# The low parts of split weights, made by GpSimd in pieces of 512 columns

## Chip, cores and metric

The kernel runs on one core of a Trainium2 chip. The metric is the device time of one execution in microseconds (us). The time before is the median of three runs; the trace is one more execution, taken by the hardware profiler. TensorE is called PE below (PEld is its weight load), VectorE is DVE, ScalarE is ACT, GpSimd is POOL, SyncE is SP.

## What is computed

Two transformer blocks stand behind one another, A and B, of two layers each, on 512 tokens of 1024 features, all in float32. Cut to what matters here:

```python
# block A, one layer
h = modulate(rms_norm(x, g1), sh1, sc1)
proj = h @ w_in                       # 1024 x 5152: queries, keys, values, gates
a = gla_chunked(...)                  # gated linear attention, two directions
b = diff_attention(...)               # softmax(p0) - lam * softmax(p1), 4 heads
x = x + g1 * ((sigmoid(ga) * (a @ w_a) + sigmoid(gb) * (b @ w_b)) @ w_o)
x = x + g2 * hier_moe(modulate(rms_norm(x, g2n), sh2, sc2))   # 32 experts, top 2
# block B, one layer
p = rmsnorm(x, n1) @ w_in             # 1024 x 2048
x = x + concat(attention, spatial_gating, conv) @ w_out
up = dwconv3(rmsnorm(x, n2) @ ffn_w_up)               # 1024 x 5632
x = x + (silu(gate) * val) @ ffn_w_down               # 2816 x 1024
```

## The kernel before

Activations lie with features on the 128 partitions and the 512 tokens along a row. The weights of a product come from HBM in **blocks** of 2 MB (128 partitions x 4096 columns of float32; the blocks of the down projection have 2816 columns, two of the up projection 2048, the first block of A 256). SP loads them into `ring`, a buffer of slots.

The large products are made in split form. A float32 matrix is written as a high part (rounded to float32r, the format that PE multiplies in one pass) and a low part, which is what the rounding dropped. PE then sums three products: high by high, low by high, high by low. For a block of weights n of these lists (`SPLIT_A` with 11 blocks for each layer of A, `SPLIT_B` with 26 for each layer of B):

- ACT makes the high part by a copy from `ring` into `parts`, slot 4 or 5 by turns (`high_part`, a copy of 3.6 us for 4096 columns), and raises `weights_high_a` or `weights_high`.
- POOL waits for that, and makes the low part: `ring` minus the high part, written over the block in its ring slot, whose name in float32r is also `parts` (`low_part`, lines 757 and 847). It raises `weights_low_a` or `weights_low`.
- PE waits for both before the first product with that block (`block_parts`).

The high part of block n waits until PE has finished block n-2, so ACT and POOL work about one block ahead of PE. Low parts of activations are made by DVE in the same way, 512 columns at a time (lines 1568, 1937, 2032, 2039).

Every engine runs a list of instructions in program order, and the order is written by hand. What stands around the low parts:

- In A, the differential attention takes 16 steps (4 heads x 4 row tiles). In step i DVE adds the bias and takes the maxima (L1685), negates them (L1688: 2 columns), and then scales step i-1 by its sums (L1693 to L1696); ACT takes the exponentials (L2208) between; PE turns the result (L1114). The products with blocks `ga` and `gb` stand between the steps. POOL also issues the DMAs of the bias tables.
- In B, the attention takes 16 steps j: PE makes the scores, DVE takes the maxima (L1975) and scales and negates them (L1977: 2 columns, two operands in SBUF), ACT takes the exponentials (L2372), PE turns them (L1409). Products with blocks `("in", 3)` and `("in", 2)` are spread over the steps; their results leave PSUM by a copy on ACT that stands behind the exponentials in ACT's list. POOL issues the DMAs of tables behind the low parts of its first two blocks (lines 852 and below), and PE waits for all of them before its first `rope_swap`.
- In the feed-forward part of B, DVE makes the hidden rows (L2048, L2049 and L2052) and their low parts (L2039), of which PE takes one after another in the first product of the down projection.

Two of the lines that the change touches, from A and from B:

```python
pool.wait_ge(weights_high_a.sem, weights_high_a.at(l, n + 1))
pool.tensor_tensor(parts[:, s, 0:size], ring[:, s, 0:size], parts[:, 4 + n % 2, 0:size].bitcast(F32),
                   ALU.subtract).then_inc(weights_low_a.sem, weights_low_a.more())
```

Of the kernel before, what the change touches and what calls it, by code (L numbers as in the profile page):

```python
# [27 lines left out]
ALU = mybir.AluOpType  # L28
ACT = mybir.ActivationFunctionType
F32R = mybir.dt.float32r  # L30
F32 = mybir.dt.float32
# [252 lines left out]
def size_b(name):  # L284

    return {"up": lambda j: 2 * P * UPS[j][1] * KD, "dn": lambda j: KF * P}.get(name[0], lambda j: SLOT)(name[1])
# [36 lines left out]
def program(nc, ctx, inp, out):  # L323
    def sb(name, shape, dt=F32):
        return ctx.enter_context(nc.sbuf_tensor("s_" + name, shape, dt))
# [12 lines left out]
    ring = sb("ring", [P, RING, SLOT])  # L338
    parts = nc.alloc_sbuf_tensor_at("s_parts", [P, RING, SLOT], F32R, offset=at)
# [119 lines left out]
    def sig(name, per, credit=0):  # L459
        return Signal(sem(name), per, credit)  # L460
# [25 lines left out]
    weights_high_a, weights_low_a = sig("a_weights_high", len(SPLIT_A)), sig("a_weights_low", len(SPLIT_A))  # L486
# [35 lines left out]
    weights_high, weights_low = sig("b_weights_high", len(SPLIT_B)), sig("b_weights_low", len(SPLIT_B))  # L522
# [21 lines left out]
    def settle(eng):  # L544

        eng.sem_inc(settled, 1)
# [123 lines left out]
    def _(pool):  # L670
        n = [0]
# [59 lines left out]
        def rows(src):  # L731
            return src.rearrange("(k p) -> k p", p=P)

        def small(signal, dst, src):
            pool.dma_start(dst, src).then_inc(signal.sem, signal.more(16))

        with pool.Fori(0, DEPTH) as l:
# [13 lines left out]
            def low_part(n):  # L751

                size = KD * 2 * RANK if n == 0 else SLOT
                s = RA.slot(SPLIT_A[n])
                pool.wait_ge(weights_high_a.sem, weights_high_a.at(l, n + 1))
                settle(pool)
                pool.tensor_tensor(parts[:, s, 0:size], ring[:, s, 0:size], parts[:, 4 + n % 2, 0:size].bitcast(F32),  # L757
                                   ALU.subtract).then_inc(weights_low_a.sem, weights_low_a.more())


            for n in range(7):
                low_part(n)

            for h in range(HEADS):
                if h >= 2:
                    low_part(5 + h)
                if h < 2:

                    pool.wait_ge(TA.done.sem, TA.done_at(l, ("o", 1, 1)))
                else:  # L770
                    pool.wait_ge(TA.by(("L", NT * (h - 1) - 1, 1)).sem, TA.freed_at(l, ("L", NT * (h - 1) - 1, 1)))
                settle(pool)
                row = rel_dram[h, 0:1, P - 1:P - 1 + REL_W]
                small(relm_in[h], relm[h % 2], bass.AP(tensor=row.tensor, offset=row.offset, ap=[[REL_N - 1, P], [1, REL_W]]))

            low_part(9)
            pool.wait_ge(TA.done.sem, TA.done_at(l, ("L", HEADS * NT - 1, 1)))
            settle(pool)
# [49 lines left out]
        with pool.Fori(0, DEPTH) as l:  # L828

            pool.wait_ge(TB.done.sem, l * TB.done.per + (TB.index[("par", 1)] + 1))  # L830
            settle(pool)
            for c in range(2):
                small(params_in_b, prow[44 * c:44 * c + 44, 0, :], rows(inp["ffn_conv_w_2"][l, c]))
            small(params_in_b, prow[0:44, 1, :], rows(inp["ffn_conv_w_2"][l, 2]))
            small(params_in_b, prow[44:52, 1, :], rows(inp["norm1_g_2"][l]))
            small(params_in_b, prow[52:60, 1, :], rows(inp["norm2_g_2"][l]))
            for r, name in ((60, "q_norm_g_2"), (61, "k_norm_g_2")):
                for c in range(2):
                    small(params_in_b, prow[r:r + 1, 1, 64 * c:64 * c + 64], inp[name][l].rearrange("(k p) -> k p", k=1))
            small(params_in_b, prow[62:68, 1, :], inp["conv_w_2"][l].rearrange("t (k p) -> (t k) p", p=P))  # L840

            def low_part(n):

                s, size = RB.slot(SPLIT_B[n]), size_b(SPLIT_B[n])
                pool.wait_ge(weights_high.sem, weights_high.at(l, n + 1))
                settle(pool)
                pool.tensor_tensor(parts[:, s, 0:size], ring[:, s, 0:size], parts[:, 4 + n % 2, 0:size].bitcast(F32),  # L847
                                   ALU.subtract).then_inc(weights_low.sem, weights_low.more())

            low_part(0)  # L850

            pool.wait_ge(TB.freed["V"].sem, TB.freed["V"].at(l, 0))
            settle(pool)
            small(tables_in, swap, inp["swap"])
            small(tables_in, sin_t, inp["rope"][1])
            small(tables_in, cos_t, inp["rope"][0])
            low_part(1)
            small(tables_in, wsr, inp["sg_w_2"][l].rearrange("h p q -> p h q"))
            for h in range(4):
                small(tables_in, bsb[64 * (h % 2):64 * (h % 2) + 64, h // 2, :], inp["sg_b_2"][l, h].partition_broadcast(64))  # L860
            small(tables_in, gvb, inp["sg_norm_g_2"][l].partition_broadcast(P))
            for n in range(2, len(SPLIT_B)):
                low_part(n)
# [1618 lines left out]
```

## Time and profile before

| | |
|---|---|
| median of three runs | 3723.69 us (3720.17 to 3726.69) |
| profiled execution | 3723.39 us, its span 3721.7 us |
| busy in the span | PE 3159.5 us (85%), DVE 1131.9 (30%), ACT 962.3 (26%), POOL 805.8 (22%) |
| mean granted clock of PE | 0.917 of full speed |
| low parts, block A (line 757) | 22 instructions, 180.4 us |
| low parts, block B (line 847) | 52 instructions, 407.8 us |
| DMA | 663.67 MB, mean 178 GB/s |

A layer of A with its experts takes about 1180 us (the attention half 0 to 615 us, the experts up to 1180), a layer of B about 655 us (2395 to 3050 and 3050 to 3700). A row of the timeline has the start in us, the time in us, the engine, the line, the operation, out<-in, the shapes and the count; in brackets the idle time of the engine ahead of it and what ended that. Rows of equal instructions that follow one another are merged. Times of PE are modelled, and an instruction's time holds the time that it waits inside the engine for its operands.

### The profile page before, as it was taken

The page shows a single profiled execution, that of the slowest core. Times are in us where ns is not written, and L with a number is a line of the kernel's source. Part 1 is how long each engine was busy: PE and PEld are TensorE (multiplying, and loading weights), DVE is VectorE, ACT ScalarE, POOL GpSimd, SP SyncE. Part 2 cuts the span into 40 slices and gives each one's busy share as a digit, 9 for nine tenths or more (in the row PEclk, how much of TensorE's full clock was granted, in tenths as well). Part 3 has the DMA queues.
Part 4 walks back from the last instruction along what each step waited for, and adds up shares of the span by engine and source line. Part 5 has one row for each costly group of instructions (what it writes and reads, how often), then busy time and mean ns, then how long its engine had stood idle before and what let it go on. Part 6 is the DMA issues. An engine that isn't in the chain of part 4 may idle for free. (4 is left out here: it accounts for less than half of the span.)

```text
span 3721.7 us, 42396 instructions
## 1 busy us (share of the span) xinstructions
PE 3159.5 (85%) x15027; PEld 2046.8 (55%) x15027; DVE 1131.9 (30%) x2001; ACT 962.3 (26%) x1351; POOL 805.8 (22%) x382
## 2 busy tenths in 40 slices
PE   6988987888884798879688777588899998889999
PEld 4764644333332576454433333365688786568877
DVE  4464423111111446431311111134343303434330
ACT  4323311111111522330111111134333323433331
POOL 3311100111111221120011111230243343024432
PEclk7998997899997899889799999789899998989999
DMA  5223332899998122332499999610122331012232
GB/s 209 68 76 126 136 115 91 340 405 409 409 408 311 69 75 99 119 114 92 180 396 408 409 409 407 256 51 31 60 91 80 90 123 51 31 61 91 80 90 69
DMA packets 289710, 663.67 MB, mean 178 GB/s; under 512 B 20190, under 2 KB 114708, under 8 KB 289552
## 3 DMA queue, kind: packets, MB, share of 16 engines
q1 hardware_dynamic: 271680, 623.43, 45.1%
q0 software_dynamic: 17872, 38.14, 2.8%
q8 instruction: 98, 1.61, 0.2%
q14 instruction: 60, 0.49, 0.0%
HBM read 653.64 MB, written 25.69 MB: 183 GB/s over the span
## 5 line engine op out<-in xcount | busy, mean ns | idle before, releaser
L869 PE MATMUL psum<-s_parts 128*128 128x512 f32 (+1 forms) x3744 | 955.2, 407 | 119.5 <-POOL s_parts L757 39.2
L869 PEld LDWEIGHTS psum<-s_parts 128*128 128x128 f32 (+1 forms) x3744 | 723.3, 195 | 327.6 <-issue 85.6
L869 PE MATMUL psum<-s_ring,s_units 128*64 128x512 f32 x3168 | 743.8, 619 | 129.8 <-DMA s_ring<-in_w_expert_in 90.9
L847 POOL TENSOR_TENSOR s_parts<-s_ring,s_parts 128x4096 fp32r<-128x4096 f32 (+2 forms) x52 | 407.8, 7841 | 873.1 <-ACT s_parts L2068 873.1
L869 PEld LDWEIGHTS psum<-s_ring,s_units 128*64 128x64 f32 x3168 | 251.4, 141 | 578.8 <-issue 446.1
L869 PE MATMUL psum<-s_h_low,s_parts 128*128 128x512 f32 (+1 forms) x1872 | 470.7, 392 | 11.2 <-DVE s_hid_low L2039 11.2
L869 PEld LDWEIGHTS psum<-s_h_low,s_parts 128*128 128x128 f32 (+1 forms) x1872 | 350.6, 188 | 96.0 <-DVE s_hid_low L2039 12.1
L869 PE MATMUL psum<-s_units 128*128 (+9 forms) x1520 | 296.5, 412 | 99.1 <-DVE s_gsl L1829 34.3
L757 POOL TENSOR_TENSOR s_parts<-s_ring,s_parts 128x4096 fp32r<-128x4096 f32 (+1 forms) x22 | 180.4, 8200 | 685.0 <-ACT s_parts L2068 685.0
L2068 ACT ACTIVATE s_parts<-s_ring 128x4096 fp32r<-128x4096 f32 (+3 forms) x74 | 237.3, 3209 | 168.4 <-PE psum L869 103.7
L869 PEld LDWEIGHTS psum<-s_units 64*128 64x128 f32 (+3 forms) x1520 | 175.3, 193 | 178.7 <-issue 121.1
L1828 DVE TENSOR_SCALAR s_put_at<-psum,s_half_row 128x1 int32<-128x1 f32 x66 | 14.4, 218 | 716.5 <-DMA ys_scratch<-s_units,s_put_at 716.5
L2068 ACT ACTIVATE s_units<-psum 128x512 f32<-128x512 f32 (+1 forms) x264 | 151.1, 599 | 260.3 <-PE psum L869 208.1
L798 POOL DMA_INDIRECT s_units<-h_scratch,s_take_at x66 | 81.9, 1241 | 591.1 <-DVE s_take_at L1823 468.4
L869 PE MATMUL psum<-s_units,s_ring 128*128 128x512 f32 x448 | 199.5, 596 | 3.5 <-DVE s_temps L1712 3.5
L2048 DVE SCALAR_TENSOR_TENSOR s_units<-psum,s_par,s_units 128x511 f32<-128x511 f32 x88 | 66.0, 750 | 280.5 <-ACT s_units L2434 280.5
L869 PEld LDWEIGHTS psum<-s_units,s_ring 128*128 128x128 f32 x448 | 83.6, 190 | 112.4 <-issue 103.7
L2272 ACT ACTIVATE s_units<-psum,s_gsl 128x512 f32<-128x512 f32 x66 | 45.4, 687 | 372.7 <-PE psum L869 372.7
L2434 ACT ACTIVATE s_units<-psum,s_par 128x512 f32<-128x512 f32 x88 | 60.7, 690 | 308.6 <-PE psum L869 308.6
L807 POOL DMA_INDIRECT ys_scratch<-s_units,s_put_at x66 | 67.0, 1016 | 328.9 <-ACT s_units L2272 295.9
L2266 ACT ACT_TABLE_LOAD x31 | 39.8, 1283 | 257.8 <-PE psum L869 257.8
L1519 DVE RECIPROCAL s_temps<-s_temps 128x512 f32<-128x512 f32 x28 | 93.9, 3353 | 19.5 <-ACT s_temps L2093 19.5
(350 smaller groups left out, 2664.4 us busy)
## 6 DMA issues: line engine op xcount, KB each, us to landing
s_ring<-in_w_expert_in SPq DMA_DIRECT2D x132, 2048.0 KB, 23.5
s_ring<-in_w_expert_out SPq DMA_DIRECT2D x66, 2048.0 KB, 24.6
s_ring<-in_w_in SPq DMA_DIRECT2D x28, 2048.0 KB, 8.8
s_ring<-in_w_ada SPq DMA_DIRECT2D x24, 2048.0 KB, 9.2
s_ring<-in_ffn_w_up SPq DMA_DIRECT2D x40, 1024.0 KB, 6.4
s_ring<-in_ffn_w_down SPq DMA_DIRECT2D x16, 1408.0 KB, 7.0
s_ring<-in_w_out SPq DMA_DIRECT2D x8, 2048.0 KB, 7.8
s_units<-ys_scratch POOLq DMA_DIRECT2D x16, 512.0 KB, 6.4
```

The costliest lines, as they stand in the source:

```text
L757: pool.tensor_tensor(parts[:, s, 0:size], ring[:, s, 0:size], parts[:, 4 + n % 2, 0:size].bitcast(F32), ALU.subtract).then_inc(weights_low ...
L798: pool.indirect_dma_start(out=xs[u % 2], out_offset=None, in_=h2_dram[:, :], in_offset=bass.IndirectOffsetOnAxis(ap=take_at[:, u % 2, 0:1] ...
L807: pool.indirect_dma_start(out=ys_dram[:, :], out_offset=bass.IndirectOffsetOnAxis(ap=put_at[:, u, 0:1], axis=0), in_=ys[u], in_offset=None ...
L847: pool.tensor_tensor(parts[:, s, 0:size], ring[:, s, 0:size], parts[:, 4 + n % 2, 0:size].bitcast(F32), ALU.subtract).then_inc(weights_low ...
L869: return pe.matmul(o, lhsT=lhsT, rhs=rhs, start=start, stop=stop)
L1519: link(ve.reciprocal(temps[:, 2, :], temps[:, 3, :]))
L1828: ve.tensor_scalar(put_at[:, u % 2, :], psum[:, 7, 1:2], 2.0, half_row[:, 0:1], ALU.mult, ALU.add).then_inc(m_put_written.sem, m_put_writt ...
L2048: link(ve.scalar_tensor_tensor(out=up_t[:, b, 1:SEQ], in0=o[:, 0:SEQ - 1], scalar=w[0], in1=up_t[:, b, 1:SEQ], op0=ALU.mult, op1=ALU.add))
L2068: return ae.activation(o, i, ACT.Copy) if scale is None else ae.activation(o, i, ACT.Copy, scale=scale)
L2266: ae.activation(sil[u], psum[:, u, 0:256], ACT.Silu).then_inc(m_silu_made.sem, m_silu_made.more())
L2272: ae.activation(ys[u], psum[:, 5 + u, :], ACT.Copy, scale=gsl[:, u:u + 1]).then_inc(m_ys_made.sem, m_ys_made.more())
L2434: ae.activation(up_t[:, n % 4, :], o, ACT.Copy, scale=par[:, col:col + 1]).then_inc(up_centre.sem, up_centre.more())
```

## The change

Both `low_part` functions issue the same subtraction in pieces of 512 columns: 8 instructions for a block of 4096 columns, 6 for 2816 (the last has 256), 4 for 2048, one for 256. The pieces stand behind one another with no wait between, on the same rows, and only the last raises the semaphore. What is computed, what waits for it, and all other engines' lists are as before.

```diff
@@ low_part of block A
-                pool.tensor_tensor(parts[:, s, 0:size], ring[:, s, 0:size], parts[:, 4 + n % 2, 0:size].bitcast(F32),
-                                   ALU.subtract).then_inc(weights_low_a.sem, weights_low_a.more())
+                for c in range(0, size, 512):
+                    cols = slice(c, min(c + 512, size))
+                    ins = pool.tensor_tensor(parts[:, s, cols], ring[:, s, cols], parts[:, 4 + n % 2, cols].bitcast(F32), ALU.subtract)
+                ins.then_inc(weights_low_a.sem, weights_low_a.more())
@@ low_part of block B
-                pool.tensor_tensor(parts[:, s, 0:size], ring[:, s, 0:size], parts[:, 4 + n % 2, 0:size].bitcast(F32),
-                                   ALU.subtract).then_inc(weights_low.sem, weights_low.more())
+                for c in range(0, size, 512):
+                    cols = slice(c, min(c + 512, size))
+                    ins = pool.tensor_tensor(parts[:, s, cols], ring[:, s, cols], parts[:, 4 + n % 2, cols].bitcast(F32), ALU.subtract)
+                ins.then_inc(weights_low.sem, weights_low.more())
```

POOL's list around the second block of B, before. The row with `s_aT<-in_sg_w` is the first of the table loads that stand behind the low part (`in_sg_b`, `in_sg_norm_g` are the rest).

```order
L735 DMA s_units<-in_rope 128x512 x2
L845 REGISTER_ALU
L847 TENSOR_TENSOR s_parts<-s_ring,s_parts 128x4096
L735 ISA
L735 DMA s_aT<-in_sg_w 128x4x128
L735 ISA
L735 DMA s_units<-in_sg_b 64x128
```

The same place after.

```order
L735 DMA s_units<-in_rope 128x512 x2
L847 REGISTER_ALU
L851 TENSOR_TENSOR s_parts<-s_ring,s_parts 128x512 x8
L735 ISA
L735 DMA s_aT<-in_sg_w 128x4x128
L735 ISA
L735 DMA s_units<-in_sg_b 64x128
```

One instruction became eight; the table loads stand behind the last of them.

## Rows read from the trace of the kernel before

**Rows 1.** The page, costliest groups: busy us, mean ns | idle before, releaser.
```profile
L847 POOL TENSOR_TENSOR s_parts<-s_ring,s_parts 128x4096 fp32r<-128x4096 f32 (+2 forms) x52 | 407.8, 7841 | 873.1 <-ACT s_parts L2068 873.1
L757 POOL TENSOR_TENSOR s_parts<-s_ring,s_parts 128x4096 fp32r<-128x4096 f32 (+1 forms) x22 | 180.4, 8200 | 685.0 <-ACT s_parts L2068 685.0
```

**Rows 2.** Lines of DVE, one answer each: count, ns min/median/max, first and last start.
```profile
L1977 DVE SCALAR_TENSOR_TENSOR s_lamv<-s_lamv x32: 160/161/8099, 2494.3 to 3268.0; 128x2 f32<-128x2 f32 x32
L1688 DVE TENSOR_SCALAR s_sc<-s_sc x32: 169/170/7730, 282.3 to 1603.0; 128x2 f32<-128x2 f32 x32
```

**Rows 3.** Timeline, block B, first layer, an early attention step.
```profile
2491.89 3.93 PE L869 MATMUL psum<-s_parts 128*128 128x512 f32 x16
...
2504.47 5.87 PE L869 MATMUL psum<-s_parts 128*128 128x512 f32 x16 [5.78 <-ACT s_units L2068]
...
2494.26 8.01 DVE L1977 SCALAR_TENSOR_TENSOR s_lamv<-s_lamv 128x2 f32<-128x2 f32 x1
...
2502.31 0.78 ACT L2372 ACTIVATE s_units<-psum,s_lamv 128x512 f32<-128x512 f32 x1 [7.84 <-DVE s_lamv L1977]
...
2493.35 8.90 POOL L847 TENSOR_TENSOR s_parts<-s_ring,s_parts 128x4096 fp32r<-128x4096 f32 x1 [22.15 <-ACT s_parts L2068]
```

**Rows 4.** A window there: length, engines' busy us (x instructions), granted clock, DMA.
```profile
2504.00:2511.00 7.00, 6.53 (x20) 5.24 (x21) 0.00 (x0) 1.94 (x5) 0.00 (x0) 0.67 0.00 0
```

**Rows 5.** Timeline, block B, a later attention step, first layer and second.
```profile
2580.64 8.10 DVE L1977 SCALAR_TENSOR_TENSOR s_lamv<-s_lamv 128x2 f32<-128x2 f32 x1
...
2591.03 5.30 PE L869 MATMUL psum<-s_parts 128*128 128x512 f32 x16 [7.53 <-ACT s_units L2068]
...
3241.84 3.78 PE L869 MATMUL psum<-s_parts 128*128 128x512 f32 x8 [9.09 <-ACT s_units L2068]
```

**Rows 6.** Timeline, block A, first layer, an attention step of the third head.
```profile
358.42 1.09 PE L1114 MATMUL psum<-s_ident,s_units 128*128 128x128 f32 x4 [6.43 <-DVE s_units L1696]
...
348.92 7.73 DVE L1688 TENSOR_SCALAR s_sc<-s_sc 128x2 f32<-128x2 f32 x1
...
357.00 0.49 DVE L1695 TENSOR_SCALAR s_units<-s_units,s_sc 128x512 f32<-128x512 f32 x1
357.52 0.75 DVE L1696 SCALAR_TENSOR_TENSOR s_units<-s_units,s_sc 128x512 f32<-128x512 f32 x1
...
347.81 8.81 POOL L757 TENSOR_TENSOR s_parts<-s_ring,s_parts 128x4096 fp32r<-128x4096 f32 x1 [44.20 <-ACT s_parts L2068]
```

**Rows 7.** Timeline, block B, first product of the down projection.
```profile
2944.34 1.22 PE L869 MATMUL psum<-s_h_low,s_parts 128*128 128x512 f32 x2 [5.62 <-DVE s_hid_low L2039]
...
2937.93 6.96 DVE L2039 TENSOR_TENSOR s_hid_low<-s_units,s_h_low 128x512 fp32r<-128x512 f32 x2 [0.73 <-ACT s_h_low L2068]
2944.81 4.89 DVE L2039 TENSOR_TENSOR s_hid_low<-s_units,s_parts 128x512 fp32r<-128x512 f32 x8
...
2953.41 1.52 PE L869 MATMUL psum<-s_units_high,s_parts 128*128 128x512 f32 x6
```

**Rows 8.** Durations of the low parts, by line: ns min/median/max, start, forms.
```profile
L847 POOL TENSOR_TENSOR s_parts<-s_ring,s_parts x52: 4597/8962/9370, 2396.7 to 3690.1; 128x4096 fp32r<-128x4096 f32 x32, 128x2816 fp32r<-128x2816 f32 x16, 128x2048 fp32r<-128x2048 f32 x4
L757 POOL TENSOR_TENSOR s_parts<-s_ring,s_parts x22: 720/8851/9194, 52.1 to 1650.3; 128x4096 fp32r<-128x4096 f32 x20, 128x256 fp32r<-128x256 f32 x2
```

**Rows 9.** Timeline of POOL: instructions with no wait between them.
```profile
0.41 0.10 POOL L2470 MEMSET const-float32-0.0<- 128x1 f32 x1 [0.41 <-issue]
0.44 0.10 POOL L2470 MEMSET const-float32-1.0<- 128x1 f32 x1
```

**Rows 10.** PE's waits: total us, times, longest us.
```profile
PE psum L869 <- POOL s_parts L757: 39.2, 8, 14.5
PE psum L869 <- POOL s_parts L847: 3.2, 2, 1.6
PE psum L869 <- DMA s_units<-in_sg_norm_g: 8.0, 2, 4.5
```

**Rows 11.** Timeline, block A: PE's first product with the first gate block.
```profile
287.49 0.72 PE L869 MATMUL psum<-s_parts 128*128 128x512 f32 x2 [1.68 <-POOL s_parts L757]
```

## The prediction

> **What bounds the kernel now.** I read the page first: POOL is busy for a fifth of the span, and all its low parts together last 588 us [rows 1]. A busy POOL costs nothing by itself, so three questions decide: who waits for a low part, who is slowed while one runs, and where of that PE is idle.
>
> The second question is answered by the lines of DVE [rows 2]. L1977 works on 2 columns. Its median is 161 ns, its longest 8099. L1688, also 2 columns, has 170 and 7730. The timeline gives the reason [rows 3]: L1977 starts at 2494.26 and ends at 2502.27, and the low part of POOL that began at 2493.35 ends at 2502.25. The same stands in [rows 6] (356.65 beside 356.62) and in [rows 7]. So a DVE instruction whose operands lie in SBUF, with two of them or in the fast one-operand form, stands still while a low part runs, and goes on when it ends. DVE instructions that read PSUM are not touched by it: L1685 and L1975 keep their times beside a low part.
>
> Then PE's gaps. In these four places of each layer pair the stall becomes PE idle time: 5.78 us [rows 3], 7.53 in the first layer and 9.09 in the second [rows 5], 6.43 [rows 6], 5.62 [rows 7]. In the first two ACT stands between: it waits for L1977 before its exponentials [rows 3], and the copy that frees a PSUM bank is queued behind them. Elsewhere (L2052, L1568, the stall of the first L1688) PE has no gap behind the stall, or one that POOL itself ends.
>
> Last, who waits for POOL's result: PE does 8 times for a low part in A, 39.2 us, that is four times a layer, and once a layer in B, 1.6 us at most; and once a layer in B for table loads that POOL issues behind the low part of its second block [rows 10].
>
> **What a piece costs.** No piece of 512 columns is in the trace. A block of 2048 takes 4597 ns and one of 256 720 [rows 8], so a column costs 3877/1792 = 2.16 ns and an instruction 0.17 us beside it. A piece alone is then 1.27 us, and eight make 10.2 us where the median is 8.96: 1.2 us more. At the other end the 0.17 us lie under the piece before; instructions with no wait between do overlap on POOL, 0.10 us long at a distance of 0.03 [rows 9]. Eight pieces are then 8 x 1.11 = 8.9 us: nothing more. Neither row is a subtraction in pieces, so I take the middle: 1.19 us a piece, 9.5 us and **0.6 us more** for a block of 4096 columns, 0.4 for one of 2816; ends 0 and 1.2.
>
> **What is lost.** Five of the six waits of a layer pair stand behind a block of 4096 columns, and one (in the down projection) behind 2816: 5 x 0.6 + 0.4 = 3.4 us. The wait at 287.49 [rows 11] loses more. There the low part runs beside the attention's first step, and DVE instructions that until now stood in its shadow will take the port between pieces: two L1688, L1694, L1695 and L1696 by their times [rows 2, 6] are 0.17 + 0.17 + 0.2 + 0.49 + 0.75 = 1.8 us, of which I take 1.3. Together 4.7 us a layer pair. A low part that nobody waits for has room: in the up projection it is ready over 4 us ahead, so its longer time costs nothing.
>
> **What is won.** I take it that POOL gives the port up at the end of each piece and that DVE, if it waits, goes next. A DVE instruction then waits for the rest of one piece, 0 to 1.2 us, and a following one that needs the port waits for a whole piece again.
>
> - *L1977 at 2494.26* [rows 3]. It ends by 2495.7. ACT's exponentials are over before PE has finished the product whose bank they free, and the gap of 5.78 goes. What is late next is the block whose low part is running: it would be ready at 2493.35 + 9.5 + 0.5 = 2503.4, and PE wants it after 24 more products of 0.246 us from 2498.7, at 2504.6 or later. It is just in time. The gap also lowered the clock: 16 products took 5.87 us behind it and 3.93 ahead of it, and the granted clock of the window behind is 0.67 [rows 4], which is a mix of the levels 1.2 and 2.4 GHz. That is 1.9 us more. Together 7.7.
> - *L1977 at 2580.64* [rows 5]. The block under way is not wanted for 40 us. The gap shrinks to about 0.5 us, and 0.8 comes back one step later, since three DVE instructions of the convolution (L2023 to L2025) and the next L1977 now each wait for a piece. 7.53 - 1.3 = 6.2 in the first layer, 9.09 - 1.3 = 7.8 in the second: 7.0 a layer.
> - *L1688 at 348.92* [rows 6]. L1688, L1694, L1695 and L1696 need the port one after another. Piece ends at 349.0, 350.4, 351.8 and 353.5 put the end of L1696 at 354.2, where it was 358.27. PE's gap goes from 6.43 to about 2.3: 4.1. That gap and the one of 4 us behind it stay, so I count nothing for the clock.
> - *L2039 at 2937.93* [rows 7]. Ten low parts of DVE stand there, and PE takes them one at a time. If they alternate with POOL's pieces, the last ends after 6.3 us of pieces and 10 x 0.61 of its own, from 2937.56: at 2950.0, no earlier than before (2944.81 + 4.89 = 2949.70). But PE gets the first ones early, needs no catching up, and ends at about 2951 and not at 2953.41. 2.0.
>
> Sum 7.7 + 7.0 + 4.1 + 2.0 = 20.8, less 4.7, is 16.1 a layer pair, and there are two: 32 us. The experts' stage between has no low parts and moves as a whole. The profiled execution took 3723.39, 0.3 under the median of the runs, so **3691.5 us** stands for both. The unfavourable ends (pieces of 1.27 us, the first place 5.8, the second 4, the third 2, the fourth 0) give 11.8 less 8.5, times two: 7 us, 3717. The favourable ones (pieces that add nothing, so a loss of 1.3, and the clock behind the second and fourth gap, 1.3 and 0.5) give 22.6 less 1.3, times two: 43 us, 3681. The forecast's own range is 3681 to 3717.
>
> **Rules of the skill.** The row shows a stall that ends with an instruction, not what happens between two that are queued. The Trainium skill, "SBUF — State Buffer", section "SBUF: two separate sides", says that the port pair is an exclusive lock, held for the whole instruction by whoever came first. By it each piece ends a hold, and the sum is the one above. The Trainium skill, "GPSIMD Engine Reference", section "Instruction dispatch", says that each of the eight cores of GpSimd starts the next instruction when its own share is done, while others still write. By it there may be no moment at which the port is free between pieces; that is the first rival.
>
> **The rivals.** *POOL keeps the port through the queued pieces.* POOL's instructions overlap when no wait stands between [rows 9], as the pieces will. Then L1977, L1688 and L2039 wait for the last piece as they do now for the end of the block, every stall is longer by what the pieces add, and so is every wait for POOL. Loss: 3.4 for the waits and 3 x 0.6 + 0.4 = 2.2 for the stalls, 5.6 a layer pair, 11 in all: 3735, up to 3746 with pieces of 1.27. It decides from the point at which the gap between pieces is shorter than what DVE needs to get in. Against it speaks that POOL must set up each instruction, and the 0.17 us of that touch no operand. Chance 0.18, of which 0.03 within 0.2% (pieces that add nothing).
>
> *DVE never has to alternate.* DVE's instructions follow each other at 0.61 us though each lasts 0.69 [rows 7], so POOL may find no way in until the row of them is over, and small ones may slip in during POOL's set-up. Then the third place gives 6.4 + 2.5 for the clock, the fourth 5.6 + 1.9, the second 8.3 + 1.3 and the first 7.7: 33.7 less 1 for waits, 65 us in all: 3658. Chance 0.12.
>
> *The low part takes the stall's place.* In the first place it is just in time, and in the third the end of L1696 hangs on four pieces; pieces of over 1.3 us, or more DVE work between them than I count, give the gain back to a wait of PE for POOL: 3717. Chance 0.08.
>
> **How the numbers follow.** Forecast 0.62 with 3681 to 3717, no alternation (or only in part) 0.12 at 3655 to 3681, POOL in the stall's place 0.08 at 3715 to 3731, port kept 0.18 at 3724 to 3746. The range 3664 to 3731 leaves out half of the second and two thirds of the last, under 0.2. A measurement of this kernel can tell 0.2%, 7.4 us, from no change. Faster by more: 0.62 + 0.12 and 0.01 of the third, 0.75. Within: 0.07 + 0.03 = 0.10. Slower: 0.15.
>
> **What would show it.** Right: L1977's and L1688's longest time near 1.2 us in place of 8; no gap of PE near 2504, one of about 2 us at the third place, small gaps between the products near 2940; POOL's pieces 1.1 to 1.3 us apart, with longer steps where DVE got in; the wait at 287.49 longer by 2 us. Wrong: one DVE instruction of 8 us across all eight pieces (port kept), pieces over 1.4 us apart with no DVE between (price too low), or L2039 in a run with no pieces between (no alternation).

## The result

| | before | after |
|---|---|---|
| median of the runs of one comparison | 3721.93 us (3714.87 to 3726.69, 4 runs) | 3695.81 us (3694.3 to 3700.32, 4 runs) |
| profiled execution | 3723.39, span 3721.7 | 3696.47, span 3694.8 |

The ratio is 0.9933, with a 95% interval of 0.9915 to 0.9952: 26 us faster, where 32 were forecast (3691.5). Kernels below are compared with runs of before in the same comparison (medians of 3721.3 to 3723.84 us).

Line numbers move by two or four: L757 is now L759, L847 is L851, L869 is L873, L1688 is L1692, L1694 to L1696 are L1698 to L1700, L1977 is L1981, L2039 is L2043, L2068 is L2072. First, the longest times of the DVE lines of [rows 2], and the low parts of [rows 8] (ns min/median/max, first and last start):

```profile
L1981 DVE SCALAR_TENSOR_TENSOR s_lamv<-s_lamv x32: 160/161/1015, 2500.9 to 3243.3; 128x2 f32<-128x2 f32 x32
L1692 DVE TENSOR_SCALAR s_sc<-s_sc x32: 168/169/1228, 287.1 to 1606.7; 128x2 f32<-128x2 f32 x32
L759 POOL TENSOR_TENSOR s_parts<-s_ring,s_parts x162: 721/1268/1738, 48.0 to 1664.0; 128x512 fp32r<-128x512 f32 x160, 128x256 fp32r<-128x256 f32 x2
```

8099 ns has become 1015 and 7730 has become 1228: about one piece. The work of POOL has grown: by the page it is busy for 891.6 us where it was 805.8 [rows 1].

```profile
L851 POOL TENSOR_TENSOR s_parts<-s_ring,s_parts 128x512 fp32r<-128x512 f32 x368 | 467.7, 1307 | 781.4 <-ACT s_parts L2072 781.3
```

So the port passes to DVE between pieces. The timeline of the place of [rows 3] shows what follows (start us, duration us, engine, line, names, count, idle before and releaser):

```profile
2499.95 10.01 POOL L851 TENSOR_TENSOR s_parts<-s_ring,s_parts 128x512 fp32r<-128x512 f32 x8 [21.14 <-ACT s_parts L2072]
2500.86 0.39 DVE L1981 SCALAR_TENSOR_TENSOR s_lamv<-s_lamv 128x2 f32<-128x2 f32 x1
2501.29 0.78 ACT L2376 ACTIVATE s_units<-psum,s_lamv 128x512 f32<-128x512 f32 x1 [0.22 <-DVE s_lamv L1981]
...
2504.17 1.13 PE L873 MATMUL psum<-s_units 64*128 64x512 f32 x4
...
2505.23 3.94 PE L873 MATMUL psum<-s_parts 128*128 128x512 f32 x16
...
2506.63 0.86 DVE L1981 SCALAR_TENSOR_TENSOR s_lamv<-s_lamv 128x2 f32<-128x2 f32 x1
```

ACT waited 7.84 us for this line and now waits 0.22. The 16 products that stood behind a gap of 5.78 us, and took 5.87, stand behind none and take 3.94. Two steps of the attention pass beside one low part. At the place of [rows 5] PE's gap of 7.53 is 1.55:

```profile
2576.99 10.98 POOL L851 TENSOR_TENSOR s_parts<-s_ring,s_parts 128x512 fp32r<-128x512 f32 x8 [67.03 <-ACT s_parts L2072]
2577.75 0.52 DVE L1981 SCALAR_TENSOR_TENSOR s_lamv<-s_lamv 128x2 f32<-128x2 f32 x1
2578.80 0.97 DVE L2027 TENSOR_SCALAR s_temps<-s_units,s_par 128x512 f32<-128x512 f32 x1
2579.80 1.63 DVE L2028 SCALAR_TENSOR_TENSOR s_temps<-s_units,s_par,s_temps 128x511 f32<-128x511 f32 x1
2580.56 3.93 PE L873 MATMUL psum<-s_parts 128*128 128x512 f32 x16 [1.55 <-ACT s_units L2072]
```

In A, at the place of [rows 6], the gap of 6.43 is 0.41 (the window shows six of the eight pieces):

```profile
354.21 8.01 POOL L759 TENSOR_TENSOR s_parts<-s_ring,s_parts 128x512 fp32r<-128x512 f32 x6 [42.89 <-ACT s_parts L2072]
355.32 0.17 DVE L1692 TENSOR_SCALAR s_sc<-s_sc 128x2 f32<-128x2 f32 x1
355.62 0.21 DVE L1698 TENSOR_SCALAR s_sc<-s_sc 128x1 f32<-128x1 f32 x1
355.87 1.11 DVE L1699 TENSOR_SCALAR s_units<-s_units,s_sc 128x512 f32<-128x512 f32 x1
357.01 1.64 DVE L1700 SCALAR_TENSOR_TENSOR s_units<-s_units,s_sc 128x512 f32<-128x512 f32 x1
358.80 0.63 PE L1118 MATMUL psum<-s_ident,s_units 128*128 128x128 f32 x4 [0.41 <-DVE s_units L1700]
```

The place of [rows 7] has many DVE operations beside one low part. In before, the one that began at 2937.93 stood still until that low part ended at 2943.74:

```profile
2937.56 6.18 POOL L847 TENSOR_TENSOR s_parts<-s_ring,s_parts 128x2816 fp32r<-128x2816 f32 x1 [7.73 <-ACT s_parts L2068]
```

In after, DVE and POOL take turns:

```profile
2925.69 9.21 POOL L851 TENSOR_TENSOR s_parts<-s_ring,s_parts 128x512 fp32r<-128x512 f32 x6 [7.02 <-ACT s_parts L2072]
2926.06 3.17 DVE L2043 TENSOR_TENSOR s_hid_low<-s_units,s_h_low 128x512 fp32r<-128x512 f32 x2 [0.74 <-ACT s_h_low L2072]
2929.15 8.70 DVE L2043 TENSOR_TENSOR s_hid_low<-s_units,s_parts 128x512 fp32r<-128x512 f32 x8
2929.29 0.74 PE L873 MATMUL psum<-s_h_low,s_parts 128*128 128x512 f32 x2 [0.74 <-DVE s_hid_low L2043]
2930.99 0.73 PE L873 MATMUL psum<-s_parts 128*128 128x512 f32 x2 [0.72 <-DVE s_hid_low L2043]
```

The six pieces of a 2816 block last 9.21 us and not 6.9, and eight DVE operations that followed each other in 4.89 us now take 8.70. As long as pieces are left, the starts of two DVE operations lie 1.70 us apart, one piece and one operation; the last four, behind the last piece, follow at 0.6 us. One gap of 5.62 us is four of 0.7.

The cost stands in PE's waits (total us, times, longest), to be read beside [rows 10]:

```profile
PE psum L873 <- POOL s_parts L759: 48.7, 8, 15.5
PE psum L873 <- DMA s_units<-in_sg_norm_g: 11.2, 2, 5.6
PE psum L873 <- POOL s_parts L851: 5.2, 4, 2.6
```

39.2 us in A became 48.7, 8.0 became 11.2, and 3.2 became 5.2. To see where the time went, I set the start of the same instruction of PE in two traces side by side (each has 15,027 of them) and took the difference to before, in us:

| point (time in before) | after | only A | only B | selected | n = 2 | waited for | unwaited |
|---|---|---|---|---|---|---|---|
| before any piece matters (44.6) | -3.9 | -1.5 | -3.9 | -1.5 | 0.1 | -1.6 | -1.7 |
| A, layer 1: ahead of the attention (159.4) | -0.5 | 2.0 | -1.3 | 1.1 | 1.1 | 1.9 | 0.8 |
| the same, 112 products on (185.2) | 4.7 | 7.1 | -1.3 | 1.1 | 6.2 | 7.1 | 0.8 |
| end of its low parts (482.1) | 4.7 | 4.9 | -1.3 | -3.7 | 5.7 | 11.2 | 0.4 |
| A, layer 2, start (1270.1) | 1.8 | 0.9 | -4.4 | -5.9 | 0.7 | 7.7 | -5.6 |
| end of its low parts (1660.3) | 5.8 | 5.0 | -4.8 | -10.2 | 9.3 | 14.9 | -2.9 |
| B, layer 1, behind its wait for tables (2450.2) | 8.0 | 6.5 | -2.6 | -9.6 | 9.8 | 14.7 | -3.0 |
| B, layer 2, start (3090.2) | -11.8 | 6.3 | -19.6 | -30.0 | 10.0 | 14.1 | 0.5 |
| near the end (3690.1) | -27.3 | 7.8 | -36.8 | -49.9 | 10.1 | 14.1 | 0.5 |

(The columns behind "after" belong to the experiments.) The kernel loses 8.6 and 4.0 us in the two layers of A. Counted from 2394.9, where B begins (it is 6.5 late there), it wins 18.3 and 15.5 in those of B, with the longer waits for the tables in both. The first row and the steps of up to 6 us in the experts' stage, which has no low parts, tell how far single executions differ by themselves.

### The profile page after: what moved, and what is told of

Read it like the earlier page. It is cut to its first block and busy times, and to the rows that moved or that the text cites. A ratio compares the mean times of both kernels' runs of the same rounds, so it can differ in the third digit from the quotient of the medians.

```text
span 3694.8 us, 42852 instructions
## 1 busy us (share of the span) xinstructions
PE 3154.5 (85%) x15027; PEld 2040.3 (55%) x15027; DVE 1099.1 (30%) x2001; ACT 962.6 (26%) x1351; POOL 891.6 (24%) x838
## 5 line engine op out<-in xcount | busy, mean ns | idle before, releaser
L873 PE MATMUL psum<-s_parts 128*128 128x512 f32 (+1 forms) x3744 | 952.0, 406 | 110.9 <-POOL s_parts L759 48.7
L873 PEld LDWEIGHTS psum<-s_parts 128*128 128x128 f32 (+1 forms) x3744 | 718.5, 194 | 320.7 <-issue 96.0
L873 PE MATMUL psum<-s_ring,s_units 128*64 128x512 f32 x3168 | 744.4, 619 | 129.9 <-DMA s_ring<-in_w_expert_in 90.4
L851 POOL TENSOR_TENSOR s_parts<-s_ring,s_parts 128x512 fp32r<-128x512 f32 x368 | 467.7, 1307 | 781.4 <-ACT s_parts L2072 781.3
L873 PEld LDWEIGHTS psum<-s_ring,s_units 128*64 128x64 f32 x3168 | 249.2, 141 | 581.4 <-issue 447.7
L873 PE MATMUL psum<-s_h_low,s_parts 128*128 128x512 f32 (+1 forms) x1872 | 468.4, 390 | 1.7 <-DVE s_hid_low L2043 1.5
L873 PEld LDWEIGHTS psum<-s_h_low,s_parts 128*128 128x128 f32 (+1 forms) x1872 | 348.9, 187 | 86.2 <-issue 9.1
L873 PE MATMUL psum<-s_units 128*128 (+9 forms) x1520 | 298.0, 413 | 98.3 <-ACT s_units L2072 35.4
L759 POOL TENSOR_TENSOR s_parts<-s_ring,s_parts 128x512 fp32r<-128x512 f32 (+1 forms) x162 | 205.6, 1304 | 668.6 <-ACT s_parts L2072 668.6
L2072 ACT ACTIVATE s_parts<-s_ring 128x4096 fp32r<-128x4096 f32 (+3 forms) x74 | 237.3, 3209 | 164.5 <-PE psum L873 99.4
L873 PEld LDWEIGHTS psum<-s_units 64*128 64x128 f32 (+3 forms) x1520 | 180.0, 197 | 175.7 <-issue 116.9
L2072 ACT ACTIVATE s_units<-psum 128x512 f32<-128x512 f32 (+1 forms) x264 | 150.8, 598 | 276.7 <-PE psum L873 224.2
L873 PE MATMUL psum<-s_units,s_ring 128*128 128x512 f32 x448 | 199.5, 596 | 3.5 <-DVE s_temps L1716 3.5
L873 PEld LDWEIGHTS psum<-s_units,s_ring 128*128 128x128 f32 x448 | 83.6, 190 | 112.4 <-issue 103.6
```

The lines of the kernel that those rows point to most:

```text
L759: ins = pool.tensor_tensor(parts[:, s, cols], ring[:, s, cols], parts[:, 4 + n % 2, cols].bitcast(F32), ALU.subtract)
L851: ins = pool.tensor_tensor(parts[:, s, cols], ring[:, s, cols], parts[:, 4 + n % 2, cols].bitcast(F32), ALU.subtract)
L873: return pe.matmul(o, lhsT=lhsT, rhs=rhs, start=start, stop=stop)
L2072: return ae.activation(o, i, ACT.Copy) if scale is None else ae.activation(o, i, ACT.Copy, scale=scale)
```

## The experiments

**Theory.** The gain is stalls of DVE that end with a piece, in B for the most part and at one place of A; the loss is that every waited-for block is ready later. **Rivals**: the gain comes from something else in the new order; or A's loss comes from the low parts that nobody waits for, through DVE work that they disturb.

**Each half alone.** Pieces only at L757 (A), and only at L847 (B): one hunk of the change's diff each.

> Pieces of 512 columns in block A alone, whole low parts in block B. By the steps of the prediction a layer of A wins 4.1 us at L1688 and loses 3.7 at the waits: no change. By the two traces, laid beside one another, a layer of A comes out 4 to 9 us longer with pieces: 3730 to 3737 us where before is 3722. If the gain had nothing to do with the places named, A would carry a third of it: 3714.

> Pieces of 512 columns in block B alone, whole low parts in block A. By the two traces B is shorter by 21 us in its first layer and 15 in the second: 3684 to 3690 us. By the prediction's own terms (16.7 won and 1.0 lost a layer) 3691. If the gain came from the first microseconds of the program, where the trace after is 3.9 us ahead before any piece runs, it would be 3700 or more.

Only A: 3733.89 us (10 runs), ratio 1.0027 (1.0016 to 1.0038), 12.6 us slower. Only B: 3686.95, ratio 0.9903 (0.9887 to 0.992), 34 us faster. The change is a gain of 34 and a loss of 13, where the prediction had 31 and nearly nothing. The two halves add up to 22 us and the change wins 26; the interval of only A reaches from 6 to 14 us, so the runs leave this difference open. The table says where A loses: of the 8.6 us of its first layer in after, 5.2 come between 159.4 and 185.2, where no wait for POOL stands. The windows there show the granted clock (length, busy us of PE, PEld, DVE, ACT and POOL with their instructions, clock, DMA), first for before:

```profile
155.00:160.00 5.00, 5.00 (x44) 4.81 (x42) 0.00 (x0) 4.70 (x3) 0.72 (x1) 1.00 0.75 241
160.00:168.00 8.00, 6.56 (x34) 4.62 (x34) 0.69 (x1) 3.30 (x5) 8.00 (x1) 0.73 0.29 111
168.00:176.00 8.00, 8.00 (x35) 6.25 (x33) 6.72 (x5) 1.96 (x4) 0.11 (x1) 0.84 0.00 0
```

The same windows in the kernel with pieces only in A show 0.56 and 0.58:

```profile
160.00:168.00 8.00, 8.00 (x42) 7.71 (x41) 0.00 (x0) 1.51 (x2) 6.91 (x6) 0.56 0.54 205
168.00:176.00 8.00, 6.56 (x21) 4.10 (x21) 2.78 (x2) 3.66 (x5) 2.93 (x3) 0.58 0.00 0
```

The two levels of the clock are 1.2 and 2.4 GHz, 0.5 and 1.00 in this column. In before the clock falls at 163.7, just behind the end of PE's products (163.5), and stays at the lower level for 6.8 us. With the pieces it falls at 161.0, while PE is busy, and stays there for 13.7 us.

**The blocks nobody waits for, and those PE waits for.** The size of the pieces depends on n, for A alone:

```diff
-                for c in range(0, size, 512):
-                    cols = slice(c, min(c + 512, size))
+                for c in range(0, size, (512 if n in (3, 4, 5, 6) else size)):
+                    cols = slice(c, min(c + (512 if n in (3, 4, 5, 6) else size), size))
```

> Pieces of 512 only for blocks 3 to 6 of A's list, for which TensorE never waits and beside which no stalled VectorE instruction keeps it idle. By the prediction this changes nothing: 3721. By the traces with pieces in A, TensorE runs at the lower clock for longer between 159 and 185 us of each layer, 3.6 to 5 us a layer, which no step of the prediction has. If these blocks bring it, 3728 to 3732; if it comes from the blocks that TensorE waits for (2, 7, 9, 10), no change.

3722.75 us (10 runs) beside 3722.92, ratio 1.0001 (0.9991 to 1.001): the price of pieces is nothing where PE does not wait. The second rival falls with it for these blocks: DVE work that they disturb costs nothing either, and the window 160 to 168 has a clock of 0.76. The same edit with `n in (2, 7, 9, 10)`, the four blocks a layer that PE waits for (`gv`, the first of `ga`, both of `gb`), and with `n == 2` (`gv`) alone, which PE waits for at 102.8 us, far ahead of the stretch at the lower clock:

> Pieces of 512 columns only in the four blocks of A per layer that TensorE waits for (n = 2, 7, 9, 10); everything else whole. Question: where the 12 us come from that pieces in all of A cost. Theory 1 (the waits alone): each of these blocks is ready 1.0 us later, the first one about 2.4 because vector instructions get in, so 5.4 us a layer, 10.8 in all: 3732, and no lower granted clock between 160 and 168 us than before (0.73). Theory 2 (a part of the loss is the stretch at the lower clock between 159 and 185 us, and an early waited-for block brings it about through the distance between the streams): 3733 to 3737 with a granted clock near 0.5 in the window 160 to 168. Rival (the blocks that nobody waits for carry the loss after all): within 2 us of 3722.

> Pieces of 512 columns only in one block of A per layer, n = 2, the first full-size one that TensorE waits for near the start; everything else whole. It stands ahead of the stretch between 159 and 185 us. If the later wait for this block brings the lower clock there about, the window 160 to 168 shows a granted clock near 0.5, and the time is 3722 + 2 x (1.0 + 3.6) = about 3731. If only the wait counts, the window shows 0.73 as before and the time is 3722 + 2 x 1.0 = 3724. If the stretch isn't bound to this block, another of the waited-for blocks does it or it falls at random.

Waited for: 3738.57 us beside 3723.84, ratio 1.0044 (1.0027 to 1.006). That is 14.7 us, over the 3732 and the 3733 to 3737 of the two theories, and more than only A loses with the same four blocks, where block 8 should give back 12: 3 us by this sum, 12.6 measured. The intervals (10 to 22 us here, 6 to 14 for only A) just leave room for both, so the size of A's loss is known to some 5 us only. Only n = 2: 3730.5 (10 runs), ratio 1.0017 (1.0007 to 1.0027): 6.7 us for one block a layer. Its own wait grows by one microsecond (start, duration, idle before and releaser; before had [0.92]):

```profile
103.89 1.42 PE L871 MATMUL psum<-s_parts 128*128 128x512 f32 x5 [1.91 <-POOL s_parts L759]
```

From there to 159.4 the difference stays at 1.1 us, and then the clock falls while PE is busy, at 160.4, and stays at the lower level until 174.0:

```profile
155.00:160.00 5.00, 5.00 (x41) 4.72 (x39) 0.00 (x0) 3.94 (x2) 0.00 (x0) 1.00 0.51 150
160.00:168.00 8.00, 8.00 (x38) 7.64 (x37) 0.00 (x0) 0.76 (x2) 7.67 (x1) 0.52 0.44 168
168.00:176.00 8.00, 6.56 (x20) 4.04 (x20) 3.66 (x2) 3.66 (x5) 1.19 (x1) 0.62 0.00 0
```

The same 28 small products, before and then here:

```profile
160.14 3.33 PE L869 MATMUL psum<-s_units 64*128 64x64 f32 x28
161.89 6.23 PE L871 MATMUL psum<-s_units 64*128 64x64 f32 x28
```

The difference goes from 1.1 to 6.2 within 112 products. So the step came with the later arrival of one block. The four kernels with n = 2 in pieces of 512 have it (clock 0.50 to 0.56 in the window 160 to 168), before (0.73) and the five others in which that block is whole don't (0.65 to 0.79). The traced execution of this kernel is the second slowest of its ten (3724 to 3738 us). It ends 10.1 us behind before, the median 6.7; with 2 us for the two waits, the clock takes about 2.3 us a layer in the median by this estimate, not 5. In the second layer the same kernel goes from 0.7 at its start to 10.1 at 1380, and the other three make a like step there. But it is no rule: with pieces of 256 columns (below) the block comes later still, and the window shows 0.80; with pieces of 1024 the first layer has the step and the second doesn't. Why a delay of 1 us, 57 us earlier, makes the clock fall sooner in unchanged work stays open. It isn't the length of the wait: the kernel with pieces in n = 3 to 6 waits 2.54 us there, since PE arrives earlier, and has no such stretch.

**Only where a stalled instruction keeps PE idle.** `512 if n == 8 else size` in A and `512 if n in (3, 4, 19) else size` in B: the blocks of [rows 6], [rows 3], [rows 5] and [rows 7].

> Pieces only for the four blocks of a layer pair beside which a stalled VectorE instruction kept TensorE idle: block 8 of A's list, blocks 3, 4 and 19 of B's. If gain and loss are separate, as the prediction adds them, the gains stay (6 in A, 8, 8 and 3 in B, 25 a layer pair) and the waits of TensorE for GpSimd go back to their old length: about 3672 us, 3665 to 3680. If the gain came from elsewhere in the pieces: 3700 to 3715.

3672.0 us, as expected: ratio 0.9852 (0.9833 to 0.9871), 49 us faster than before and 24 faster than after. Its PE waits for POOL in A for 41.1 us, not 48.7:

```profile
PE psum L873 <- POOL s_parts L759: 41.1, 8, 14.5
PE psum L873 <- DVE s_hid_low L2043: 7.6, 12, 0.7
```

Gain and loss of the change are separable, since they sit at different blocks. The four blocks were split together; what each of them is worth is read from the traces, not from runs of its own.

**The stalled instruction in another form.** Low parts whole as in before; the two lines with 2 columns become two instructions of one column each:

```diff
-ve.tensor_scalar(sc[:, 12 + 2 * b:14 + 2 * b], sc[:, 8 + 2 * b:10 + 2 * b], -1.0, None, ALU.mult).then_inc(...)
+ve.tensor_scalar(sc[:, 12 + 2 * b:13 + 2 * b], sc[:, 8 + 2 * b:9 + 2 * b], -1.0, None, ALU.mult)
+ve.tensor_scalar(sc[:, 13 + 2 * b:14 + 2 * b], sc[:, 9 + 2 * b:10 + 2 * b], -1.0, None, ALU.mult).then_inc(...)
...
-ve.scalar_tensor_tensor(out=few[:, 156 + b:158 + b], in0=few[:, 152 + b:154 + b], scalar=-1.0, in1=few[:, r:r + 2],
-                        op0=ALU.mult, op1=ALU.mult).then_inc(...)
+ve.tensor_scalar(few[:, 156 + b:157 + b], few[:, 152 + b:153 + b], few[:, r:r + 1], -1.0, ALU.mult, ALU.mult)
+ve.tensor_scalar(few[:, 157 + b:158 + b], few[:, 153 + b:154 + b], few[:, r + 1:r + 2], -1.0, ALU.mult, ALU.mult).then_inc(...)
```

> GpSimd as before, whole low parts. The two small VectorE instructions that stalled are written so that they need not hold the port that GpSimd uses: L1688 (2 columns) and L1977 (2 columns, two SBUF operands) become two instructions of one column each, with the second operand of L1977 as a per-partition scalar. In the trace after, instructions of one column (L1694 there) ran in 0.21 us beside running pieces. Theory, a port held by GpSimd and wanted only by certain forms of VectorE: the stalls of 8 us at three of the four places go with no piece at all, 6 + 8 + 8 us a layer pair, about 3677 us, and no instruction of either line lasts over 0.3 us. Rival, GpSimd stops every VectorE instruction whose operands are in SBUF: no change, 3722, with stalls of 8 us.

3695.43 us, ratio 0.9924 (0.9906 to 0.9943): as fast as the change, but 18 us short of what I expected. The one-column forms are never held, yet in A the stall moves to the next instruction that needs the port:

```profile
348.81 8.83 POOL L757 TENSOR_TENSOR s_parts<-s_ring,s_parts 128x4096 fp32r<-128x4096 f32 x1 [44.16 <-ACT s_parts L2069]
350.22 0.15 DVE L1688 TENSOR_SCALAR s_sc<-s_sc 128x1 f32<-128x1 f32 x1
350.35 0.16 DVE L1694 RECIPROCAL s_sc<-s_sc 128x2 f32<-128x2 f32 x1
350.54 0.21 DVE L1695 TENSOR_SCALAR s_sc<-s_sc 128x1 f32<-128x1 f32 x1
350.79 7.13 DVE L1696 TENSOR_SCALAR s_units<-s_units,s_sc 128x512 f32<-128x512 f32 x1
358.86 1.09 PE L1114 MATMUL psum<-s_ident,s_units 128*128 128x128 f32 x4 [5.92 <-DVE s_units L1697]
```

PE's gap is 5.92 where it was 6.43: in A nothing is won. In B both gaps go, but L2024 inherits the stall and gives back a part (PE waits 2.48 us for the next copy of ACT):

```profile
2572.19 7.59 DVE L2024 TENSOR_SCALAR s_temps<-s_units,s_par 128x512 f32<-128x512 f32 x1
2585.36 1.09 PE L1409 MATMUL psum<-s_ident,s_units 128*128 128x128 f32 x8 [2.48 <-ACT s_units L2069]
```

This also shows which forms are held. `tensor_scalar` on 2 or 512 columns of SBUF is; on one column it is not, and RECIPROCAL is not. The Trainium skill, "VectorE: DVE Perf Modes", section "What auto-detection actually checks", names as conditions of the mode that uses both ports a single source and a destination in SBUF whose outermost dimensions larger than one are both even or equal. One column has no such dimension, and I read it as outside that mode; the trace agrees, with 0.15 to 0.21 us for one column beside a running low part. The section speaks neither of one column nor of RECIPROCAL.

**Both together.** The one-column lines, and pieces for n = 8 in A and n = 4 and 19 in B.

> Both remedies where each is the better: the two small VectorE instructions in one-column form as in e4_one_column, and pieces of 512 only for block 8 of A's list and blocks 4 and 19 of B's. Against the kernel with selected pieces (3672.0) block 3 of B is one instruction again, and L1977 waits for nothing: 0 to 4 us less, 3668 to 3672.

3673.25 us, ratio 0.9868 (0.9851 to 0.9884): no better than pieces at the same places alone. Once the port is given up every 1.2 us, what a 2-column instruction still waits is too little to be measured.

**Larger and smaller pieces.** 1024 and 256 columns in both lines in place of 512.

> Pieces of 1024 columns in all low parts. In the trace after, seven more instructions made a low part about 1.0 us longer, 0.14 each. With three more it is 0.4 longer, so the six waits of a layer pair cost 0.5 less each: 6 us less in all. A stalled instruction waits up to 2.2 us in place of 1.2; at the two places in B there was room, at the third (A) L1688, L1695 and L1696 wait for up to two pieces more than before, 2 us a layer. Near 3693 us, 3688 to 3698. If shorter holds were what counts, clearly slower than with 512: over 3700.

> Pieces of 256 columns. Sixteen instructions make a low part 15 x 0.14 = 2.1 us longer than one, 1.1 longer than eight; six waits a layer pair: 13 us more than with 512, less what shorter holds give at the third and fourth place (1 us each a layer): about 3707 us, 3702 to 3713. If the hold's length were what counts: 3690 or less.

1024: 3696.14 us, ratio 0.9926 (0.991 to 0.9943). 256: 3702.95, ratio 0.9955 (0.9938 to 0.9972). From 512 to 1024 the time is the same because two things cancel (both have the stretch at the lower clock in the first layer, 0.50 and 0.55 in the window 160 to 168). With 1024 a waited-for block loses less (PE's waits in A 42.9 us), but DVE instructions pay for longer turns at two places. At that of [rows 7] the kernel wins 0.8 to 1.0 us a layer where 512 wins 2.5, and at that of [rows 6] PE has a gap of 3.65 us again:

```profile
352.82 9.90 POOL L759 TENSOR_TENSOR s_parts<-s_ring,s_parts 128x1024 fp32r<-128x1024 f32 x4 [42.88 <-ACT s_parts L2072]
353.93 1.26 DVE L1692 TENSOR_SCALAR s_sc<-s_sc 128x2 f32<-128x2 f32 x1
355.54 2.22 DVE L1699 TENSOR_SCALAR s_units<-s_units,s_sc 128x512 f32<-128x512 f32 x1
357.80 2.71 DVE L1700 SCALAR_TENSOR_TENSOR s_units<-s_units,s_sc 128x512 f32<-128x512 f32 x1
360.65 0.63 PE L1118 MATMUL psum<-s_ident,s_units 128*128 128x128 f32 x4 [3.65 <-DVE s_units L1700]
```

With 256 that gap is gone, and the waits in A are 56.5 us; the stretch is absent too (0.80), which spares this kernel a part of what its waits cost.

But with 256 columns the port isn't handed over at every boundary. Seven of the 44 instructions of L2056 (the hidden rows; ns min/median/max below) stood for 3.3 us while five or six pieces passed them, and went on behind the last piece of the block:

```profile
L2056 DVE TENSOR_TENSOR s_units<-s_units x44: 691/693/4030, 2691.8 to 3558.1; 128x512 f32<-128x512 f32 x44
2756.60 3.98 DVE L2056 TENSOR_TENSOR s_units<-s_units 128x512 f32<-128x512 f32 x1
2755.82 4.22 POOL L851 TENSOR_TENSOR s_parts<-s_ring,s_parts 128x256 fp32r<-128x256 f32 x6
```

All seven began within 0.1 us of the start of a piece, but L1692 and L1981, which did so too, waited for one piece only (0.5 us). This is what the prediction's first rival describes. It cost nothing here, since PE doesn't wait for the hidden rows at these places: between 2700 and 2930, where three of the seven lie, the difference to before stays the same. With 512 and 1024 columns no DVE instruction waited longer than one piece (1.1 and 2.2 us at most). Why the hand-over failed with 256 stays open.

The durations of all 52 low parts of 4096 columns, from the start of the first piece to the end of the last, give the price of a piece. The shortest was not disturbed by DVE; the medians include some that were:

| pieces of a 4096 block | shortest | median |
|---|---|---|
| 1 | 8.81 us | 9.03 |
| 4 (1024 columns) | 9.25 | 9.47 |
| 8 (512) | 9.82 | 10.32 |
| 16 (256) | 10.95 | 11.22 |

By the shortest it is 1.01 us for 7 more instructions and 2.14 for 15: 0.14 us each, in a straight line.

## Why the prediction was right

The time (3695.81) lies in the forecast's own range of 3681 to 3717, 4 us behind the number. Step by step:

- **The port passes between pieces, and DVE goes next**: right. The longest hold of a DVE instruction fell from 7.9 to 1.1 us, and the operations of L2043 and the pieces take turns. Of the rivals, "POOL keeps the port" would have shown one DVE instruction across all eight pieces, and "DVE never has to alternate" a row of L2043 at 0.61 us; the trace shows neither: beside pieces they start 1.70 us apart. The rule behind the first (the Trainium skill, "GPSIMD Engine Reference", section "Instruction dispatch") left room for a port that is never free; here it is free between pieces of 512 that no wait separates. That rules the rival out for this size only: with pieces of 256 it happened seven times. "The low part takes the stall's place" didn't happen: the 16 products behind L1981 have no gap.
- **A piece**: the forecast was 1.19 us and 0.6 more a block; it is 1.23 and 1.0, inside the ends of 0 and 1.2. Its mistake was the middle between [rows 8] and [rows 9]: of the 0.17 us of an instruction only 0.03 lie under the piece before, and the two memsets did not stand for it.
- **The losses by waits**: 4.7 us a layer pair was forecast. In the first layer the wait at 102.8 grew from 0.92 to 3.52: 1.0 by the pieces (the kernel n = 2) and 1.6 because PE arrives earlier, as it also does with pieces only in B (2.56). The other three grew by 1.0 to 1.1, the four of the second layer by 0.9 to 1.0. The one at 287.49 [rows 11] is among them (2.79 where it was 1.68); 0.6 and 1.3 for DVE work had been put there, so the sum was too high there and too low at the others. The tables of B, at 0.6 in the forecast, cost 2.0 and 1.2: 3.59 and 4.45 us became 5.59 and 5.64. Behind them stand two low parts, not one. The down projection lost 1.0 and 0.4, and a new gap of 0.3 stands at its first block. In all about 7.
- **Places 1 and 2** (L1977): 14.7 a layer was forecast as 7.7 and 7.0. From 2495.2 to 2600.0 after wins 18.4 us in the first layer, and 15.0 at the same place of the second; with pieces only in B it is 16.7 in both. In the first layer 7.5 of the 18.4 come at the first place and 7.6 at the second, 5.9 and 6.3 at the gaps and the rest behind them, at the higher clock. That clock was counted for the first place (1.9) and held back as a favourable end for the second (1.3); the trace shows it there too. The other 3.3 us lie near 2536 and 2577, where before runs for 3.4 us each at the lower level and after doesn't. The kernel with pieces only in A runs there at the full level too, so these 3.3 can't be put down to the pieces in B.
- **Place 3** (L1688): 4.1 was forecast, 5.1 and 6.2 came in the two layers. The failed step is "L1688, L1694, L1695 and L1696 need the port one after another": L1694 works on one column and isn't held (0.21 us), and L1688 came at the end of a piece and got through in 0.17, so two instructions paid for turns and not four. PE's gap went to 0.41, not 2.3.
- **Place 4** (L2039): 2.0 was forecast by alternation, with the last low part no earlier. The alternation is what the trace shows; the gain is 3.0, and 2.5 with the new gap ahead of it.
- **What wasn't in the sum**: the longer time at the lower clock in A between 159 and 185 us and at the like place of the second layer, 5 us each in this trace, behind the wait for n = 2. The steps priced the clock at the gaps that go, and at none of the waits that grow. In this trace the term is 10 us, over a third of the gain; by the median of the ten runs with n = 2 alone it is nearer 5.

So the parts of the sum: A was to win 0.4 a layer and lost 8.6 and 4.0 (of the 8.6, some 2.5 stand in the kernels without pieces at n = 2 as well: they too reach the wait at 102.8 earlier than before did, and wait longer); B was to win 15.7 and won 18.3 and 15.5. The mechanism held, but that the total came out within 4 us is luck: the errors had opposite signs and cancelled. The price was forecast too low, and so were most gains.

## What to carry to other kernels

A long GpSimd operation locks out DVE's instructions with two operands in SBUF, and the fast ones with one, down to 2 columns. Split it where the timeline shows a stalled DVE instruction behind which PE is idle, and leave it whole where PE waits for its result: here the choice by block is worth 49 us, pieces everywhere 26. Changing the form of the stalled instruction moved the stall to the next one that needs the port, so look down DVE's list first. And a microsecond added to a wait can cost more than a microsecond if TensorE's clock falls sooner behind it; read the granted clock of the stretches after each wait, not only the wait.

## What the runs showed of the hardware

- A GpSimd subtraction of 128 x 4096 float32 takes 8.8 us in one instruction, and 0.14 us more for each further instruction it is split into. With pieces of 512 and 1024 columns a waiting DVE instruction gets the port at the next boundary although no wait stands there: the longest hold is 1.1 and 2.2 us. With pieces of 256 seven DVE instructions were passed by five or six pieces and held for 3.3 us.
- When DVE and GpSimd both have work queued that needs the port, they alternate one for one with pieces of 512: DVE operations that follow each other at 0.61 us alone start 1.70 us apart, and six pieces take 9.21 us where 6.9 is their time alone.
- `tensor_scalar` on 128 x 1 is never held beside a running low part (0.15 to 0.21 us), on 128 x 2 it was held for 7.7 us. RECIPROCAL on 128 x 2 is not held (0.16).
- One wait longer by 1.0 us was followed, 57 us later and in work that had not changed, by a granted clock of 0.52 where it was 0.73, and cost 5 us within 26. It did so in the traces of four kernels of four with pieces of 512 at that block, in both layers; with pieces of 1024 in the first layer only, and with pieces of 256 in neither. The mechanism is open.
